# Masks of two query blocks in one product, and five reordered steps, in a two-block fp32 kernel

## What is computed

```python
mem_n = rms_norm(mem, mem_norm)
h = x
for i in range(2):
    hn = rms_norm(h, norm_pre[i])
    mkv = mem_n @ w_mem_kv[i]                  # keys and values of the memory, 4 heads of 64
    proj = hn @ (w_in_a if i == 0 else w_in_b) # queries, keys, values, memory queries, gate
    main = causal softmax attention, 12 heads  # i == 0: low-rank q and kv, rotary; i == 1: forget gates
    mem_out = softmax attention over the 256 memory tokens, 4 heads
    y = concat(main, mem_out) * silu(gate)
    h = h + rms_norm(y @ w_out[i], norm_post[i])
```

## Time and profile before

| | |
|---|---|
| median of three runs | 2020.9 us |
| the profiled execution's own time | 2023.0 us |
| its span | 2021.3 us, 23916 instructions |
| TensorE busy | 1959.0 us (97%), 9938 products |
| TensorE weight loads (beside products) | 1543.3 us (76%) |
| VectorE busy | 1031.0 us (51%) |
| GpSimd busy | 784.7 us (39%) |
| ScalarE busy | 766.9 us (38%) |
| DMA | 205.71 MB, 102 GB/s in the mean |
| mean granted TensorE clock | 0.991 of full speed |

### The profile page before, as it was taken

How to read it: one execution, slowest core, us unless ns; L and a number is a source line. 1 busy time by engine, 2 the same in 40 slices (tenths; PEclk the granted TensorE clock), 3 DMA queues, 4 the chain that set the end, 5 groups by cost and what they waited for, 6 DMA issues and landing times.

```text
span 2021.3 us, 23916 instructions
## 1 busy us (share of the span) xinstructions
PE 1959.0 (97%) x9938; PEld 1543.3 (76%) x9938; DVE 1031.0 (51%) x1529; ACT 766.9 (38%) x1171; POOL 784.7 (39%) x347
## 2 busy tenths in 40 slices
PE   7999999999999999999999999999999999999998
PEld 5875666788767698977788888877977877788776
DVE  5325577556776748733566646664911343311323
ACT  5333664422364432165433223324376333312331
POOL 2232553334464452213244334344433433444342
PEclk9999999999999999999999999999999999999999
DMA  7223103356402152121334543453440222233221
GB/s 237 85 58 79 57 1 115 105 169 188 146 1 84 63 179 92 63 63 42 105 125 143 165 150 125 130 157 95 138 131 24 72 84 95 68 105 119 76 74 60
DMA packets 203404, 205.71 MB, mean 102 GB/s; under 512 B 12023, under 2 KB 199675, under 8 KB 203296
## 3 DMA queue, kind: packets, MB, share of 16 engines
q1 hardware_dynamic: 200809, 200.31, 31.2%
q0 software_dynamic: 1472, 3.72, 0.7%
q10 hardware_dynamic: 1015, 0.16, 0.1%
HBM read 201.20 MB, written 2.11 MB: 101 GB/s over the span
## 4 chain that ended last, share of the span: by engine, by line
PE 76%; DVE 8%; POOL 7%; ACT 6%; issue 2%; DMA 1%; ACTq 0%; DVEq 0%; SPq 0%
PE bank L540 43%; PE bank L1125 16%; POOL wl L2341 6%; ACT wh L1336 3%; PE bank L781 2%; PE bank L481 2%; DVE conv L2225 1%; PE bank L805 1%; PE bank L948 1%; DVE conv L2227 1%; PE bank L830 1%; DVE conv L2223 1%; PE bank L1183 1%; PE bank L1193 1%; DVE acc L1777 1%
## 5 line engine op out<-in xcount | busy, mean ns | idle before, releaser
L2341 POOL TENSOR_TENSOR wl<-ring,wh 128x2048 fp32r<-128x2048 f32 (+4 forms) x146 | 620.0, 4247 | 962.0 <-ACT wh L1336 960.3
L1336 ACT ACTIVATE wh<-ring 128x2048 fp32r<-128x2048 f32 (+4 forms) x146 | 256.0, 1754 | 298.1 <-PE bank L1125 129.9
L1777 DVE SCALAR_TENSOR_TENSOR acc<-ring,cs,acc 128x256 f32<-128x256 f32 x336 | 281.3, 837 | 12.0
L540 PE MATMUL bank<-xfh,wh 128*128 128x512 f32 x704 | 277.1, 394 | 7.0 <-POOL wl L2341 7.0
L540 PE MATMUL bank<-xfh,wl 128*128 128x512 f32 x704 | 274.3, 390 | 0.0
L540 PE MATMUL bank<-xfl,wh 128*128 128x512 f32 x704 | 274.0, 389 | 0.0
L540 PEld LDWEIGHTS bank<-xfh,wh 128*128 128x128 f32 x704 | 132.1, 188 | 42.0 <-POOL wl L2341 11.6
L540 PEld LDWEIGHTS bank<-xfh,wl 128*128 128x128 f32 x704 | 132.1, 188 | 27.9
L540 PEld LDWEIGHTS bank<-xfl,wh 128*128 128x128 f32 x704 | 132.2, 188 | 26.5
L1125 PE MATMUL bank<-hsph,wh 128*128 128x512 f32 x352 | 138.8, 394 | 2.3 <-POOL wl L2341 2.3
L1125 PE MATMUL bank<-hsph,wl 128*128 128x512 f32 x352 | 137.7, 391 | 0.0
(11 more groups left out here) (407 smaller groups left out, 4117.1 us busy)
## 6 DMA issues: line engine op xcount, KB each, us to landing
ring<-in_ada_w SPq DMA_DIRECT2D x48, 1024.0 KB, 5.3
ring<-in_ffn_w_in SPq DMA_DIRECT2D x44, 1024.0 KB, 5.1
ring<-in_w_in_b SPq DMA_DIRECT2D x14, 1024.0 KB, 5.3
ring<-in_even_w_in SPq DMA_DIRECT2D x14, 1024.0 KB, 5.1
ring<-in_ffn_w_out SPq DMA_DIRECT2D x16, 768.0 KB, 4.4
ring<-in_odd_w_in SPq DMA_DIRECT2D x12, 1024.0 KB, 6.0
ring<-in_ffn_w_out SPq DMA_DIRECT2D x16, 640.0 KB, 4.1
ring<-in_w_out SPq DMA_DIRECT2D x8, 1024.0 KB, 5.3
```

Of the source, the lines that this page charges most:

```text
L540: mm = eng.matmul(o, l_, r_, start=(first and i == 0), stop=(last and i == 2))
L1336: eng.activation(wh[:, m % SPLIT, h:w], ring[:, n % RING, h:w], ACT.Copy).then_inc(wh_ready, 1)
L1777: ins = eng.scalar_tensor_tensor(out=s, in0=w[:, k, :], scalar=cs[:, k:k + 1], in1=s, op0=ALU.mult, op1=ALU.add)
L2341: eng.tensor_tensor(wl[:, m % SPLIT, h:w], ring[:, n % RING, h:w], wh[:, m % SPLIT, h:w].bitcast(F32), ALU.subtract).then_inc(wl_ready, 1)
```

## The change

Five edits. In `scores` the first query block of the bank (0, 1) gets no mask product of its own; the one behind the second block is broadcast to two squares, columns 0 to 127 and 256 to 383 of the bank. The warming products around the memory norm become three and seven. GpSimd adds no tile of the residual in block one (l = 0), and so goes straight to the low part of in_b.f; with l = 1 it adds tiles 1, 3, 5 as before. ScalarE makes the high part of the first v chunk ahead of its last root of block one and not behind it. VectorE does the first of four ada steps right behind emptying f and not behind the scan.

```diff
--- before.py
+++ after.py
@@ -74,7 +74,7 @@
 VEC_TILES = 4
 
 
-SHARED = (1, 3, 5)
+SHARED = ((), (1, 3, 5))
 SPLIT_AT, _at = {}, 0
 for _n, _k in [("mem", 8), ("x_a", 8), ("cq", 3), ("ckv", 2), ("y_a", 8), ("x_b", 8), ("y_b", 8), ("x_even", 8),
                ("y_even", 8), ("x_ffn0", 8), ("ffn0/0", 12), ("ffn0/1", 10), ("x_odd", 8), ("y_odd", 8),
@@ -668,9 +668,9 @@
                 group_sums(sq[:, i % 2, M:2 * M], range(2), False, k == 3).then_inc(sq_used, 1)
                 counts["sq"] += 1
             counts["hn"] += 1
-            warm(2, n=S // 2)
+            warm(3, n=S // 2)
             norm_spread((mem_normed, KT), 2)
-            warm(2, n=S // 2)
+            warm(7, n=S // 2)
 
             for _ in range(2 * DEPTH):
                 chunks.append("mem")
@@ -780,8 +780,14 @@
                             if h < HEADS:
                                 eng.matmul(b[:, at_col:at_col + n], qf[0:kd, h, i * P:n], kf[0:kd, h, 0:n],
                                            start=first, stop=False, skip_group_check=True)
-                                mm = eng.matmul(b[:, at_col + i * P:at_col + n], identb[:, :], causal[:, :],
-                                                start=False, stop=last, skip_group_check=True)
+                                if not last:
+                                    continue
+                                if len(blocks) > 1:
+                                    o = b[:, 0:4 * P].rearrange("p (d c) -> p d c", c=P)[:, 0:3:2, :]
+                                    mask = causal[:, :].unsqueeze(1).to_broadcast([P, 2, P])
+                                else:
+                                    o, mask = b[:, at_col + i * P:at_col + n], causal[:, :]
+                                mm = eng.matmul(o, identb[:, :], mask, start=False, stop=True, skip_group_check=True)
                             else:
                                 g_ = h - HEADS
                                 rows = slice(HD * (g_ % 2), HD * (g_ % 2) + HD)
@@ -1509,14 +1515,16 @@
                 split_weights(tile_chunk[index[(stage, KT - 1)]] + 3)
                 root()
                 for t in range(KT):
-                    if t in SHARED:
-                        act.wait_ge(x_shared, l * len(SHARED) + SHARED.index(t) + 1)
+                    if t in SHARED[l]:
+                        act.wait_ge(x_shared, SHARED[l].index(t) + 1)
                     else:
-                        act.wait_ge(x_added, l * (KT - len(SHARED)) + t + 1 - sum(u < t for u in SHARED))
+                        act.wait_ge(x_added, l * KT + t + 1 - sum(u < t for u in SHARED[l]))
                     if l == 0:
                         eng.activation(xb[0][:, t, :], x[:, t, :], ACT.Copy, scale=vec("norm_pre", KT + t)
                                        ).then_inc(xh_ready, 1)
                     square(x[:, t, :])
+                if l == 0:
+                    split_weights(tile_chunk[index[("in_b.gate", 0)]] + 3)
                 root()
 
             out_first(0)
@@ -2006,7 +2014,7 @@
                         eng.scalar_tensor_tensor(out=xb[1][:, t - 2, :], in0=x[:, t - 2, :], scalar=vec("norm_pre", KT + t - 2),
                                                  in1=xb[0][:, t - 2, :].bitcast(F32), op0=ALU.mult, op1=ALU.subtract
                                                  ).then_inc(xl_ready, 1)
-                    if 1 <= t <= KT and t - 1 not in SHARED:
+                    if 1 <= t <= KT and t - 1 not in SHARED[l]:
                         dve.wait_ge(post_scaled, l * KT + t)
                         eng.tensor_tensor(x[:, t - 1, :], x[:, t - 1, :], o1[:, t - 1, :], ALU.add
                                           ).then_inc(x_added, 1)
@@ -2030,6 +2038,7 @@
             for t in range(2):
                 empty_scaled(("in_b.gate", t), gate[:, t, :])
             empty_scaled(("f",), frow[0:HEADS, 0, :], slice(0, HEADS))
+            ada_steps(1)
 
             def log_sigmoid(z, t, lf, s_log):
 
@@ -2042,7 +2051,7 @@
             chain.link(eng.memset(fr[5], 1.0))
             chain.link(eng.tensor_tensor_scan(fr[3], fr[5], fr[2], 0.0, ALU.mult, ALU.add))
             eng.tensor_scalar(fr[4], fr[3], -1.0, None, ALU.mult).then_inc(frows_ready, 1)
-            ada_steps(4)
+            ada_steps(3)
             for t in range(2):
                 empty_scaled(("in_b.qm", t), qm[:, t, :])
             for t in range(2, KT):
@@ -2364,13 +2373,11 @@
 
             def residual(l):
 
-                for t in SHARED:
+                for t in SHARED[l]:
                     pool.wait_ge(post_scaled, l * KT + t + 1)
                     eng.tensor_tensor(x[:, t, :], x[:, t, :], o1[:, t, :], ALU.add).then_inc(x_shared, 1)
 
             attention(0)
-            low_weights(tile_chunk[index[("out_a", KT - 1)]] + 2)
-            residual(0)
             low_weights(tile_chunk[index[("out_a", KT - 1)]] + 3)
 
             pool.wait_ge(xl_ready, SPLIT_AT["x_b"] + KT)
```

## The result

Four runs of the changed kernel gave 2000.07 to 2002.26 us, median 2001.39, beside 2020.69 us for the kernel before (four runs): a ratio of 0.9902 [0.9885, 0.9919], 19.3 us less. Forecast were 12.6 us less, and 2004.5 was the low end of the range. The profiled execution took 2000.67 us. A later set of runs gave 2002.10 against 2021.40 us, 0.9901 [0.9886, 0.9916].

A forecast was written before the change was run, and what follows sets the result against it. TensorE, busy 97% of the span, was taken to bound the kernel. Terms of 2.0 + 1.8 + 1.0 + 1.4 + 6.4 = 12.6 us off 2020.9 gave 2008.3 us, range 2004.5 to 2012.5.

The forecast's parts named there:

- Start: Kernel start: more warming products shrink TensorE's hole, so the 48 memory products run at full clock; 2.0 us (0.3 to 2.0).
- Masks: Scores of both attentions: merging two masks saves 0.09 us a head, 20 heads counted; 1.8 us (0 to 2.6).
- my small price at the joints: Scores of a head: 0.01 to 0.02 us comes back at each of the two joints after merging the masks.
- Rival two: The clock falls at the start after all, or the masks give nothing: 2010.1 us, both 2011.8; chance 0.15.
- rival four: Scores, 24 heads: the broadcast mask product is slow; decides from 0.53 us each, 2032 us at 1.1; chance 0.03.
- rival five: Scores: weight loads are not hidden at short products, so each of 24 removed masks saves 0.10 us more: 2005.9; chance 0.02.
- Residual and split: Block two: VectorE's chain shortens, 1.0 us (0.5 to 1.5); an earlier high part shortens the wait before v's products, 1.4.
- The ada step: Block two: an earlier load of the third v chunk closes a 3.9 us hole and keeps the clock; 6.4 us (5.5 to 6.4).
- Rival three: Block two: the third v chunk still comes late, products wait about 1 us, the clock may fall: 2012.0 us; chance 0.09.
- rival six: Whole kernel: masks and warming are neutral and only block two moves: 2012.1 us; chance 0.06.
- rival one: Attention one, first head: VectorE gets 0.03 us ahead of GpSimd, TensorE's holes shrink about 2 us: 2006.3; chance 0.20.
- two low stretches: Low clock at the start's memory products, 2.0 us, and behind the hole at block two's third v chunk, 2.7 us.

## Why the prediction was off

Against the first two profiled executions (2023.0 and 2000.67, 22.3 us apart) each step can be set beside its measure.

**Start, 2.0:** 1.9 us between the memory products and the turning of x (12.9 less 11.0). Besides, this execution began its memory products 1.0 us earlier (20.75 and 21.78), which is no term of mine. The hole is 1.28 us, within the 0.6 to 1.4; the clock stayed, in all six profiled executions with the new warming. The 48 products took 11.17, not 11.04. Right.

**Masks, 1.8:** 15 periods at 0.11 are 1.65 us. The heads at the start of attention one give some 0.4 more (17.5 us to the first product with v, beside 17.8 in the run that has the old masks and the port for VectorE), those of attention two 0.1 (20.7 beside 20.8): 2.1 in all. A head gives 0.11 where I had 0.09; my small price at the joints isn't seen in the periods. The broadcast costs nothing beyond its 256 columns. Rival two is out, at the start as here, and so is rival four (0.11 us where it needed 0.53). So is rival five: with 0.10 us for each mask's load in the path a head would have given some 0.20. So the rule in the Trainium skill that a weight load overlaps products in flight only when the row groups differ ("TensorE: Matmul & The Clock Gate", Part 3) is again at odds with what is measured here.

**Residual and split, 1.0 + 1.4:** 2.7 us from the gates to the first v product, and 1.1 and 1.6 one by one. Right. **The ada step, 6.4:** 6.0. The sum of this term was loose: its hole of 3.9 us (up to 405.78) counts in the four short products of the ada sums (L530), which start at 401.94 and stay. TensorE sat idle for 3.35 us, and 3.35 + 2.7 is about the 6.0 measured, where 3.9 + 2.7 would have been 6.6 and not 6.4. The path was as forecast: the load at 378.32 here is 386.4 in the time of the kernel before (8.1 us are won by the gates), forecast near 387; the slack ahead of the third v chunk is 1.2 us, forecast 0.8. Rival three and rival six are out.

The terms together: 1.9 + 2.1 + 2.7 + 6.0 = 12.7, forecast 12.6. That they agree to 0.1 is partly luck, as masks, residual and split gave a little more and the ada step a little less. What failed are two steps beside them, both put at nothing in the sum.

**The port, rival one.** I gave it a chance of 0.20, because "0.03 us is within the scatter of one start". That step was wrong: the chain of scores, maxima and low part repeats so exactly that the order is the same in every execution looked at, and the arithmetic that put VectorE 0.03 us ahead (it came out at 0.03 to 0.04) should have decided. The page "SBUF — State Buffer" of the Trainium skill, "Who interferes with whom", has the rule, that the engine which issues first keeps the shared pair for its whole instruction; the rows on either side agree (0.17 and 4.51 us). The price was mis-sized as well: 2.0 forecast, 2.9 in the marks without the masks' share (20.7 and 17.8), 2.5 in time when given to the kernel before, and 5.6 in time when taken from the changed kernel, where the hole let the clock fall. The low end of my range was no help: 2006.3 less the 0.8 for masks at 0.11 is 2005.5, not 2004.5.

**The clock outside the terms.** My sum counted two low stretches, 4.7 us. Before's profiled execution had more that I took as given, and set against nothing: at 104, 674, 879 and 1319 us. By the stretches of the table (the first of them in its second row; from the row of 134.1 and 131.9 the masks' 0.9 is taken off) they were worth 1.3 + 1.3 + 1.7 + 1.8 = 6.1 us, and an entry that was 1.0 us later adds to it. 12.7 + 2.9 + 6.1 + 1.0, less 0.3 in the last stage, are the 22.4 us between the two spans (2021.3 and 1998.9). Part of this is luck, which the medians take back: before's execution lay 2.3 us above its median, and the changed one 0.7 below its own.

How much is left in the mean can be read from the granted clock of all timed runs. A clock of 0.993 in the mean over 2019 us is 0.007 x 2019 = 14 us of work at full speed that weren't granted, at most. Worked out run by run this is 13.4 us for the 38 runs of the kernel before and 4.3 for eight of the changed one: 9.2 us less, where the sum had 4.7. So about 4.5 us, an upper bound, are clock that my terms didn't name. Which edit brings them is shown in part. The fall behind 404 us is in all seven profiled executions with the old place of the ada step and in none of the seven with the new one. The fall near 104 us is in all eight without the new warming, and in two of six with it. The others come and go on either side, but at the same places in the work: the one near 674 (652 to 658 in the changed kernels) in eight of the fourteen, the one near 1319 in five, the one near 879 in two. The one near 353 costs little: 23.7 us up to the first v product with it, 23.5 without. Why the same hole lets the clock fall in one execution and not in the next, I couldn't settle; with it stays open which part of those 4.5 us would last in another kernel.

The median, then: 2020.9 less 12.7 for the terms and 2.9 for the port is 2005.3. The 2001.4 measured leaves 3.9 us for the clock, which the upper bound of 4.5 allows. The other side (slower) had no support in any run.

## What to carry to other kernels

Where two engines meet at a shared port within some hundredths of a microsecond, work out which comes first and take the answer as the forecast; then fix the order with a wait on the one that can afford it, which here also let the six and nine covering products shrink to five and six. Price a closed hole with the low clock that follows it, and count the low stretches of several executions of the kernel before, not of one, since two profiled executions of it differed by 7 us. An edit that brings work forward ahead of a late transfer gives nothing until the transfer moves too: cost such edits in the order in which they release each other.

## What the runs showed of the hardware

A bf16 product of 256 columns that reads one 128-column tile twice through a broadcast and writes two squares 128 columns apart takes 0.11 us, where a plain one of 128 columns takes 0.06 or 0.07. The order of VectorE and GpSimd at 0.03 us was the same in 11 executions (VectorE behind with the old masks, ahead with the new), while the granted clock differed between executions of the same code at the same stretch (1.00 and 0.56 from 101 to 103 us), worth 2.7 us.
